# The scan's running decay sums: from TensorE matmuls with a broadcast weight to rows in DRAM, loaded broadcast into a ring of two quarter slots

## The reference, cut to what matters

```python
acs = jnp.cumsum((dt * a_neg).reshape(b, nc, q, g, e), axis=2)
diff = acs[:, :, :, None] - acs[:, :, None, :]
lmat = jnp.exp(jnp.where(tril, diff, -jnp.inf))
cb = jnp.einsum('bclgn,bcsgn->bclsg', cm, bm)
y_diag = jnp.einsum('bclsg,bclsge,bcsgep->bclgep', cb, lmat, xdt)
```

## Time and profile before

| | |
|---|---|
| median of 3 runs | 2171.91 us (2169.57 to 2172.75) |
| the profiled execution | 2172.42 us, of which span 2170.6 us |
| TensorE (PE) busy | 2029.3 us, 93% of the span |
| VectorE (DVE), ScalarE (ACT), GpSimd (POOL) busy | 990.8, 755.5, 237.5 us |
| the prompt scan | from 1499 to about 1798 us |

### The profile page before, as it was taken

The page is one execution under the profiler, slowest core; times in us unless marked ns, Lnnn a source line. Parts: engine busy times, 40 slices in busy tenths (PEclk is TensorE's granted clock), DMA queues, the critical chain, the costliest instruction groups (busy, mean ns, idle before and its releaser), DMA issues.

```text
span 2170.6 us, 35280 instructions
## 1 busy us (share of the span) xinstructions
PE 2029.3 (93%) x14555; PEld 1929.4 (89%) x14555; DVE 990.8 (46%) x1948; ACT 755.5 (35%) x1635; POOL 237.5 (11%) x358
## 2 busy tenths in 40 slices
PE   5999999999989999999999789999999979969997
PEld 5899999999889999999999679759999969969997
DVE  5214676525454445343346871103444465454423
ACT  5223354223443323233645112305364553132202
POOL 1000112100001011112123000001111111100000
PEclk9999999999999999999999888999999989989998
DMA  6211233211112121212266665483333545554422
GB/s 211 88 42 60 80 91 90 82 46 51 37 32 66 38 66 47 77 63 67 87 196 193 209 209 161 165 297 110 108 117 101 163 145 179 166 183 136 137 82 104
DMA packets 166992, 248.76 MB, mean 115 GB/s; under 512 B 19701, under 2 KB 114613, under 8 KB 166805
## 3 DMA queue, kind: packets, MB, share of 16 engines
q1 hardware_dynamic: 144576, 179.51, 26.5%
q0 software_dynamic: 22256, 66.98, 9.1%
HBM read 179.74 MB, written 66.70 MB: 114 GB/s over the span
## 4 chain that ended last, share of the span: by engine, by line
PE 75%; DVE 9%; ACT 6%; DMA 5%; issue 4%; SPq 0%; DVEq 0%; POOL 0%; ACTq 0%; POOLq 0%
PE bank L2236 19%; PE bank L2237 18%; PE bank L2238 18%; PE bank L2432 2%; DMA acc<-acc_T 2%; PE bank L2407 2%; DVE w_lo L1698 2%; PE bank L2538 1%; PE bank L2390 1%; PE bank L2648 1%; PE bank L2368 1%; ACT soft L1512 1%; DVE softT L1950 1%; PE bank L2471 1%; ACT Lm L1625 1%
## 5 line engine op out<-in xcount | busy, mean ns | idle before, releaser
L2236 PE MATMUL bank<-w_hi,hT_hi 128*128 128x256 f32 (+1 forms) x1848 | 534.5, 289 | 3.4 <-DVE hT_lo L2106 3.4
L2237 PE MATMUL bank<-w_lo,hT_hi 128*128 128x256 f32 (+1 forms) x1848 | 522.7, 283 | 0.0
L2238 PE MATMUL bank<-w_hi,hT_lo 128*128 128x256 f32 (+1 forms) x1848 | 521.9, 282 | 0.0
L2236 PE MATMUL bank<-hT_hi,w_hi 128*128 128x352 f32 x1344 | 458.3, 341 | 6.3 <-DVE acc L2083 5.7
L2238 PE MATMUL bank<-hT_hi,w_lo 128*128 128x352 f32 x1344 | 444.7, 331 | 0.0
L2237 PE MATMUL bank<-hT_lo,w_hi 128*128 128x352 f32 x1344 | 444.4, 331 | 0.0
L2236 PEld LDWEIGHTS bank<-w_hi,hT_hi 128*128 128x128 f32 (+1 forms) x1848 | 347.5, 188 | 4.9 <-issue 3.6
L2238 PEld LDWEIGHTS bank<-w_hi,hT_lo 128*128 128x128 f32 (+1 forms) x1848 | 348.6, 189 | 0.6
L2237 PEld LDWEIGHTS bank<-w_lo,hT_hi 128*128 128x128 f32 (+1 forms) x1848 | 347.6, 188 | 0.7
L2236 PEld LDWEIGHTS bank<-hT_hi,w_hi 128*128 128x128 f32 x1344 | 263.6, 196 | 16.7 <-issue 7.5
L2237 PEld LDWEIGHTS bank<-hT_lo,w_hi 128*128 128x128 f32 x1344 | 264.1, 197 | 1.1
(11 more groups left out here) (417 smaller groups left out, 2993.9 us busy)
## 6 DMA issues: line engine op xcount, KB each, us to landing
w_raw<-in_w_in SPq DMA_DIRECT2D x96, 512.0 KB, 4.9
kvring<-in_cache_win_kv SPq DMA_DIRECT2D x120, 256.0 KB, 3.6
feat_T<-fstage POOLq DMA_DIRECT2D x40, 528.0 KB, 3.8
fstage<-feat_T SPq DMA_DIRECT2D x16, 528.0 KB, 4.4
xc<-feat_T SPq DMA_DIRECT2D x8, 1024.0 KB, 5.8
kvring<-in_cache_mem_kv SPq DMA_DIRECT2D x28, 256.0 KB, 3.8
o_rows<-obuf POOLq DMA_DIRECT2D x48, 132.0 KB, 2.0
mo<-o_rows SPq DMA_DIRECT2D x24, 264.0 KB, 3.9
```

What stands on the lines that cost most here:

```text
L2236: pe.matmul(out, xh(k), wh(k), start=(k == 0), stop=False)
L2237: pe.matmul(out, xh(k), wl(k), start=False, stop=False)
L2238: ins = pe.matmul(out, xl(k), wh(k), start=False, stop=(k == nk - 1))
```

## The change

The running sums of the prompt chunks are made once more, turned: one matmul with `dA` as weight and `upper` as moving operand gives 128 rows (chunk and head) by 128 tokens. VectorE copies them to `yraw`, SP stores them to a DRAM tensor `sum_T` and waits until they have landed, in its place in the list (`ssd_dA`). A quarter of a chunk is four rows of 512 bytes. SP loads each quarter broadcast over 128 partitions (256 KB) into one of two slots in SBUF, `sums`: the first two at once, each further one when ScalarE's Relu has read the slot (`s_ddf`). The Relu reads `sums` instead of PSUM. The 128 prompt matmuls of L2628 go; the sample chunk keeps its own. The transposes of q = 6 no longer wait for the Relu, but for the copy of x out of the same banks (`s_dxt`), which is earlier.

```diff
+        def sum_landed(i):
+            x = 3 + i % NSUM
+            return s_kv[x], 16 * (key_loads(x) + len(range((x - len(sets)) % NRING, len(values), NVAL)) + i // NSUM + 1)
...
+            def load_sums(i):
+                if i >= NSUM:
+                    sp.wait_ge(s_ddf, i - NSUM + 1)
+                sp.dma_start(sums[:, i % NSUM, :, :].rearrange("p h l -> p (h l)"),
+                             sumT[4 * i:4 * i + 4, :].rearrange("h l -> (h l)").partition_broadcast(P)).then_inc(sum_landed(i)[0], 16)
...
+                elif s[0] == "ssd_dA":
+                    late_free(sp)
+                    sp.wait_ge(s_s0, 4)
+                    first, count = value_sem(NRING), value_landed(len(values) - 1 - (len(values) - 1 - NRING) % NVAL)
+                    sp.dma_start(sumT, yraw[:, 0:P]).then_inc(first, 16)
+                    sp.wait_ge(first, count + 16)
+                    for i in range(NSUM):
+                        load_sums(i)
+                elif s[0] == "ssd" and s[2] in (1, 2) and s[1] < NB:
+                    for i in range(4 * s[1] + 2 * s[2] - 2 + NSUM, 4 * s[1] + 2 * s[2] + NSUM):
+                        if i < 4 * NB:
+                            load_sums(i)
...
-                            act.wait_ge(s_dD, 4 * c + qq + 1)
+                            if c < NB:
+                                act.wait_ge(*sum_landed(4 * c + qq))
+                                later = sums[:, (4 * c + qq) % NSUM, :, :]
+                            else:
+                                act.wait_ge(s_dD, qq + 1)
+                                later = D_of(c, qq)
...
                     dve.wait_ge(s_ft, 1)
+                    dve.tensor_copy(yraw[:, 0:P], bank[7][:, P:2 * P])
...
+                    pe.matmul(bank[7][:, P:2 * P], dA[:, 0:P], table("upper"), start=True, stop=True)
...
-                    elif q in (1, 2):
-                        up = (table("upper") if c < NB else table("upper_s"))[0:m, 0:m]
+                    elif q in (1, 2) and c == NB:
+                        up = table("upper_s")[0:m, 0:m]
...
                         if c < NB - 1:
-                            pe.wait_ge(s_ddf, 4 * c + 8)
+                            pe.wait_ge(s_dxt, c + 2)
```

More of the change, by code:

```diff
@@ L438, in build_program @@
         zrow = dram("z_rows", [TOK, D])
+        sumT = dram("sum_T", [NB * SH, P])
         zarow = dram("z_att_rows", [TOK, AW])
@@ L525, in build_program @@
         area.close()
-        NRING, NVAL = 6, 9
+        NRING, NVAL, NSUM = 6, 9, 2
         area = ExitStack()
@@ L561, in build_program @@
         yraw = sb(area, "yraw", [P, TOK])
+        last = ExitStack()
+        sums = sb(last, "sums", [P, NSUM, 4, P])
+        last.close()
         yst2 = sb(area, "yst2", [P, KT8, NS])
@@ L569, in build_program @@
         yraw2 = sb(area, "yraw2", [P, TOK])
+        sb(area, "above_sums", [P, 96])
         acc1 = sb(area, "acc1", [P, TOK])
@@ L1624, in _ @@
                             for h in range(4):
-                                ins = act.activation(l[:, h, :], D_of(c, qq)[:, h, :], ACT.Relu, scale=-1.0,
+                                ins = act.activation(l[:, h, :], later[:, h, :], ACT.Relu, scale=-1.0,
                                                      bias=sc[0:m, 2, SH * c + 4 * qq + h:SH * c + 4 * qq + h + 1])
```

## The result

| | us, median (range, runs) | ratio to before [95%] |
|---|---|---|
| before | 2172.33 (2169.57 to 2176.25, 4) | |
| after | 2210.36 (2205.95 to 2213.57, 4) | 1.0158 [1.0121, 1.0194] |

The change makes the kernel 1.6% slower. Forecast were 2184 us and a range of 2168 to 2200: the direction was right, the size was outside the range. The profiled execution of after took 2205.95 us, with a span of 2204.2 against 2170.6 of before, so 33.6 us have to be found.

A forecast was written before the change was run, and what follows sets the result against it. Two paths of nearly one length were taken to bound each chunk: TensorE's work and the chain to the masked quarters. 12.8 + 0.8 + 15 + 1.5 - 18.3 = +11.8 us on 2171.9 gave 2184 us, range 2168 to 2200.

The forecast's parts named there:

- the price of the lower clock: Chunks 1 to 7: TensorE's work after the new idle time runs at half clock, 2.1 us a chunk, 15 us slower.
- the chain: From L2612 to L2648: copies, norm, w_hi split, four Relu and Exp pairs and mask take 18.7 us.
- TensorE's early arrival: Ahead of L2648 in chunks 1 to 7: TensorE's own work is 15.3 us, so it idles some 3.4 us.
- The gain: Removed L2628 matmuls and waits: each chunk gains at most TensorE's slack ahead of L2648, 18.3 us in all.
- The Relu out of SBUF: ScalarE's Relu reading SBUF instead of PSUM: no difference; bound 1 us a chunk less, 8 in all.
- The start: Chunk 0: SP waits for the sums before loading xc, so TensorE's transposes start 12.8 us later; bounds 10.1 and 14.2.
- The ring: Quarter loads into two slots: no wait in chunks 1 to 5, 1.5 us for chunks 6 and 7 together.
- That the clock does not fall: Rival for the idle ahead of L2648: full clock holds, 15.8 us less, 2168 us; chance 0.15.
- That TensorE is the bound: Rival: chain shorter than TensorE's own 15.3 us, matmuls and waits come off whole, some 29 us less, 2143; chance 0.06.
- That the ring binds: Rival: quarter loads take 3.8 us or more, every chunk waits 1 to 2 us, 8 to 16 more, 2196; chance 0.14.
- That the start is hidden: Rival at chunk 0: the late xc costs nothing, 2171 us, no change; chance 0.03.
- the likeliest case: The forecast itself: 2184 us, slower by 0.5%, own range 2176 to 2193; chance 0.62.

The follow-up runs named there:

- the kernel with the start alone: Kernel before plus turned sums made, stored, awaited by SP ahead of xc, two quarters loaded but unread; scan keeps its matmuls: 2190.93 us, 1.0091.
- the one with xc first: Kernel after, but SP issues chunk 0's xc and zt before waiting for, storing and loading the sums: 2195.03 us, 1.0115.
- the kernel with its useless matmuls: Kernel after, but TensorE still makes the 128 broadcast matmuls, which nobody reads; the Relu reads the loaded sums: 2193.46 us, 1.0101.
- one projection moved: Kernel before, with one projection step in each of chunks 1 to 5 moved ahead of the Lm matmuls: 2189.37 us, 1.0094.
- the kernel with the first move: Kernel after with chunk 0's xc ahead of the sums and, in chunks 1 to 5, one projection step moved ahead of the Lm matmuls: 2168.04 us, 0.9979.

## Why the prediction was right in direction and wrong in size

**The term that was mis-sized is the price of the lower clock.** The prediction found the chain, its length (18.7 us), TensorE's early arrival (3.4 us; measured 3.5 to 4.3 in chunks 1 to 5, but 10.36 and 6.48 in chunks 6 and 7, for which it said 3.4 too) and that the clock would fall. It priced the fall at 2.1 us a chunk, 15 us in all, at most 20, from stretches of 3.0 and 6.5 us at clock 0.50. Measured: 3.4 to 5.6 us a chunk, 32.9 us in all. Those two rows were not all that before has at the lower clock in the scan, and not the longest. Chunk 4 has one of 6.8 us and chunk 6 one of 10.2 us; inside them:

```profile
1660.00:1666.50 6.50, 4.69 (x19) 0.52 0.00 1
1739.20:1749.00 9.80, 5.92 (x23) 0.50 0.55 197
```

Two shorter examples were taken for the bounds, though in after the clock stayed at 0.50 for 13.4 us in chunk 1 and 10.2 in chunk 2. And what a stretch costs is half of what TensorE is busy in it: 5.92 of 9.80 us in this one of before, which also had slack behind it, but 9.68 of 10.20 us in chunk 2 of after, where it falls on dense work. The wider bound could have been had from rows on record: the Lm matmuls behind the idle time take 3.68 us and the matmuls behind them go at the same clock until it is granted again, so doubling L2648 alone gives 3.7 us a chunk, 26 us over seven, above the 20.

**The gain was put at 18.3 us and was 10.6.** Chunk 0: 2.9 instead of 3.9; chunks 1 and 5: 0.2 instead of 1.3; chunks 2 and 3: 0.05 instead of 0.67; chunk 4: 6.5 instead of 7.6; chunk 6: 1.6 instead of 2.2; chunk 7 0.9 worse, where 0.67 better was forecast. The rule used, that a chunk gains no more than its slack, was right; the chain was taken as unchanged and grew, by 0.6 us in chunks 2 and 3 and by 1.0 to 1.1 in chunks 1, 4 and 5, in which ScalarE also waits for a load. The Relu out of SBUF was taken at the price of that out of PSUM, with a bound only on the cheaper side. It takes 386 ns in the median:

```profile
L1659 ACT ACTIVATE Lm<-sums,sc x128: 352/386/413, 1527.3 to 1811.9; 128x128 f32<-128x128 f32 x128
```

The row it leaned on, 294 ns for an Exp without that bias, was another instruction, and its 354 ns for L1625 are a mean that the small Relus of the sample group pull down: those of 32x32 take 262 ns, and the median of before is 365.

**The start was put at 12.8 us, at most 14.2, and was 16.1.** Its order was as written, step by step. The store of 64 KB landed after 4.2 us, not after 2.2 as POOL's did nor after the 2.15 given beside it, and after 4.1 in the kernel with the start alone and in the one with xc first; xc took 10.0, near the 9.8 of its bound. The lower clock behind it was taken at 0.8 us on top; chunk 0's window is 0.6 longer than where xc comes first (20.83 against 20.19). What was not priced: the 528 KB store of `feat_T` that POOL issues at 1501.65, ahead of the turned sums in the DMA engines. It stands 0.3 us ahead in all eight kernels that make the store, so that it is the cause of the 4.2 us was not tried.

**The ring** was put at 1.5 us and costs 2.3 us of ScalarE's waits, the longest 0.9. It does not bind every chunk, as the rival had it; but its waits of 0.4 us in chunks 1, 4 and 5 and of 0.9 in chunk 7 lie on the chain and are part of the gain that stayed out.

**The rivals.** That the clock does not fall fell with the rows of chunk 1. That TensorE is the bound fell with the waits of 36.2 us. That the ring binds would have been 8 to 16 us and was 2.3. That the start is hidden fell with the idle time of 17.65 us. The range of 2168 to 2200 took its upper edge from the one with the ring; what came was the likeliest case with a dearer clock, for which no case had been written.

**The rule of the clock.** The Trainium skill, page "TensorE: Matmul & The Clock Gate", section "HAM oscillation — how this bites in real kernels", describes a loop whose matmuls wait for operands once per step and so start every step at the lower clock. This case's traces agree in all seven chunks that have the wait, and the kernel with its useless matmuls shows the other side of it.

**By the sum:** 12.8 became 16.1 and 15 became 32.9. The 0.8 of the start's lower clock (measured 0.6), the 1.5 of the ring and the slower Relu all lie in the windows and show in the 10.6 that 18.3 became. That is +38.4 us for what the prediction spoke of. Ahead of the scan are 2.8 more, 0.6 of it for the added matmul and copy, and behind it 7.5 less; 2.1 and 7.5 of these are unchanged code.

## What to carry to other kernels

Where TensorE's slack at a wait is shorter than the work that is taken away, the rest becomes idle time, and the price of idle time is read not at the wait but in the work behind it: assume the whole next group of matmuls at half clock, not the shortest stretch that the trace happens to show. Take work off TensorE only together with other work for the same place, and look at what that work's evictions stand ahead of on ScalarE. A load that waits for a store goes behind every load that the next stage needs first.

## What had not been expected of the hardware

- The stretch at the lower clock had very different lengths for nearly equal idle times: 13.4 us behind 4.32 us of idle time in chunk 1, 10.2 behind 3.64 in chunk 2, 6.8 behind 3.49 in chunk 4, and in chunk 6, without the change, 10.2 us in before and 20.5 with one projection moved. Idles of 0.47 to 0.75 us were followed by no fall.
- Unchanged code ahead of the scan takes different time in different executions. The scan began at 1499.25 us in before and at 1510.55 in before with the projection moved, with nothing different ahead of it; with the sums made but xc first it began at 1500.85, 1506.96, 1507.32, 1507.77 or 1512.70. The granted clock differs there at the same work. 1275 to 1350 us, before and then the kernel with the first move:

```profile
1275.00:1350.00 75.00, 69.68 (x448) 67.12 (x449) 26.22 (x37) 15.12 (x31) 1.06 (x2) 0.84 0.57 177
```

```profile
1275.00:1350.00 75.00, 69.65 (x404) 66.75 (x403) 28.77 (x41) 14.09 (x29) 1.06 (x2) 0.77 0.55 171
```

  Why the clock differs there stays open. The totals go with it: of the 16 later runs of before the fastest took 2162.45 us at a mean clock of 0.970 and the slowest 2180.54 at 0.960. That is why the scan was compared by its own marks.
- Four Relus of 128x128 with their bias take 1.26 us out of SBUF and 1.12 out of PSUM.
- The 64 KB store from SP landed after 3.8 to 4.2 us in the eight executions that make it, moved or not; those of the same size from POOL took 2.2.
